# Prompt values of one attention pair: one full-array product per key block in place of two column-half products

## What is computed

```python
def sparse_attend(q, k_sel, v_sel, q_pos, k_pos, rel_bias):
    logits = jnp.einsum('bthd,btkhd->bhtk', q, k_sel).astype(jnp.float32) * ATTN_SCALE
    ...
    p = jax.nn.softmax(logits, axis=-1).astype(v_sel.dtype)
    out = jnp.einsum('bhtk,btkhd->bthd', p, v_sel)
    return out.reshape(q.shape[0], q.shape[1], D_ATTN)
```

## Time and profile before

| | |
|---|---|
| three executions | 1859.91, 1866.31, 1863.84 us; median 1863.84 |
| profiled execution | span 1871.8 us from the first to the last instruction; what lies around the span is not shown by its profile |
| TensorE busy | 1726.3 us (92%) |
| VectorE, ScalarE, GpSimd busy | 859.4, 653.4, 603.9 us |
| stage with the changed line | 539 to 966 us of the span |

### The profile page before, as it was taken

One profiled execution on the slowest core, in us unless ns is written; L12 is line 12 of the kernel. 1 busy time (PEld: TensorE's weight loads), 2 busy tenths in 40 slices (PEclk: granted clock), 3 DMA queues, 4 the chain that ended last, 5 costly groups with the idle time before them and its releaser, 6 DMA issues.

```text
span 1871.8 us, 28982 instructions
## 1 busy us (share of the span) xinstructions
PE 1726.3 (92%) x11176; PEld 1413.1 (75%) x11176; DVE 859.4 (46%) x1839; ACT 653.4 (35%) x1374; POOL 603.9 (32%) x715
## 2 busy tenths in 40 slices
PE   7888999989967778898789999999999999999998
PEld 6553464789944455565555689999999999999997
DVE  4571889757734444566531343323132323232324
ACT  4464786577232233343321121222222222222123
POOL 1100334266354665555513140404040404040400
PEclk9799999989987899998889999999999999999999
DMA  8301202111184655655571001111110101020202
GB/s 242 93 1 49 92 31 78 49 35 42 43 270 149 177 173 160 175 152 152 149 260 66 0 1 46 46 46 45 39 50 29 60 20 70 10 80 3 98 1 96
DMA packets 68965, 158.03 MB, mean 84 GB/s; under 512 B 9402, under 2 KB 25518, under 8 KB 68608
## 3 DMA queue, kind: packets, MB, share of 16 engines
q1 hardware_dynamic: 47488, 84.91, 13.7%
q0 software_dynamic: 21376, 71.75, 12.8%
HBM read 144.14 MB, written 12.49 MB: 84 GB/s over the span
## 4 chain that ended last, share of the span: by engine, by line
PE 82%; DVE 6%; issue 4%; another core or an unknown queue 3%; ACT 3%; POOL 2%; DMA 1%; SPq 0%; DVEq 0%; ACTq 0%; POOLq 0%
PE psum L1819 7%; PE psum L1817 7%; PE psum L1806 7%; PE psum L1807 7%; PE psum L1805 7%; PE psum L1818 7%; PE psum L1746 6%; PE psum L1360 5%; PE psum L1524 4%; PE psum L1373 3%; PE psum L1549 2%; PE psum L1663 2%; PE psum L1340 2%; PE psum L1641 2%
## 5 line engine op out<-in xcount | busy, mean ns | idle before, releaser
L1805 PE MATMUL psum<-n_hi,wup_hi 128*128 128x384 f32 (+1 forms) x768 | 251.3, 327 | 0.0
L1817 PE MATMUL psum<-h_hi,wdn_hi 128*128 128x384 f32 (+1 forms) x768 | 250.9, 327 | 0.0
L1807 PE MATMUL psum<-n_hi,wup_lo 128*128 128x384 f32 (+1 forms) x768 | 250.8, 327 | 0.0
L1806 PE MATMUL psum<-n_lo,wup_hi 128*128 128x384 f32 (+1 forms) x768 | 250.8, 327 | 0.0
L1819 PE MATMUL psum<-h_hi,wdn_lo 128*128 128x384 f32 (+1 forms) x768 | 250.2, 326 | 0.0
L1818 PE MATMUL psum<-h_lo,wdn_hi 128*128 128x384 f32 (+1 forms) x768 | 250.1, 326 | 0.0
L2441 DVE TENSOR_TENSOR h_lo<-h_full,h_hi 128x384 fp32r<-128x384 f32 (+1 forms) x96 | 112.5, 1184 | 261.5 <-ACT h_hi L1221 252.8
L1213 ACT ACTIVATE hrelu<-psum 128x384 f32<-128x384 f32 (+1 forms) x96 | 45.5, 474 | 502.0 <-PE psum L1807 502.0
L2446 DVE TENSOR_TENSOR x_region<-psum,x_region 128x384 f32<-128x384 f32 (+1 forms) x192 | 102.8, 536 | 252.9 <-PE psum L1819 251.8
L905 POOL TENSOR_TENSOR wup_lo<-wup_full,wup_hi 128x4096 fp32r<-128x4096 f32 x8 | 72.3, 9037 | 421.0 <-ACT wup_hi L1197 421.0
L1075 ACT ACTIVATE arena<-x_region,arena 128x384 bf16<-128x384 f32 (+2 forms) x192 | 166.5, 871 | 23.3 <-POOL arena L851 23.3
(11 more groups left out here) (329 smaller groups left out, 3155.1 us busy)
## 6 DMA issues: line engine op xcount, KB each, us to landing
wup_full<-in_w_up SPq DMA_DIRECT2D x8, 2048.0 KB, 8.0
wdn_full<-in_w_down SPq DMA_DIRECT2D x8, 2048.0 KB, 7.7
arena<-in_x_prompt SPq DMA_DIRECT2D x16, 512.0 KB, 8.8
arena<-in_w_in SPq DMA_DIRECT2D x3, 2048.0 KB, 8.4
arena<-in_w_in SPq DMA_DIRECT2D x12, 512.0 KB, 5.6
out<-arena SPq DMA_DIRECT2D x17, 256.0 KB, 4.5
arena<-in_w_out SPq DMA_DIRECT2D x8, 512.0 KB, 8.4
out<-arena SPq DMA_DIRECT2D x8, 512.0 KB, 2.7
```

Of the source, the lines that this page charges most:

```text
L1805: pe.matmul(b, wu_hi[:, k, col], n_hi[:, k, o:o + w], start=(k == 0), stop=False)
L1806: pe.matmul(b, wu_hi[:, k, col], n_lo[:, k, o:o + w], start=False, stop=False)
L1807: i = pe.matmul(b, wu_lo[:, k, col], n_hi[:, k, o:o + w], start=False, stop=(k == KT - 1))
L1817: pe.matmul(b, wd_hi[:, f, col], h_hi[:, hf, 0:w], start=(f == 0), stop=False)
```

## The change

For each key block of a pair there is one product: the 128 value columns of both heads as weights, and the 2 x 128 queries of both heads as moving columns, into all 128 partitions and 256 columns of bank 3. Of the four quarters of the result two are a head's own (partitions 0 to 63 with columns 0 to 127, partitions 64 to 127 with columns 128 to 255); the other two pair one head's values with the other head's probabilities and are not read. `take_values` copies the two own quarters, with one copy each. `pv_done` counts one a pair, and the waits on it are adapted.

```diff
@@ sync engine: loads of the output weights
-            sp.wait_ge(pv_done, 2 * NPR)
+            sp.wait_ge(pv_done, NPR)
@@ def even_turn(q, e), ScalarE
-                act.wait_ge(pv_done, 2 * q)
+                act.wait_ge(pv_done, q)
@@ def values(q), TensorE
                 for k in range(i_ + 1):
-                    for e in range(2):
-                        i = pe.matmul(bank(3)[64 * e:64 * e + 64, 0:P], V[:, k, (2 * hp + e) * HD:(2 * hp + e + 1) * HD],
-                                      probT[:, e, k, :], start=(k == 0), stop=(k == i_), skip_group_check=True)
-                        if k == i_:
-                            i.then_inc(pv_done, 1)
+                    i = pe.matmul(bank(3)[:, 0:2 * P], V[:, k, 2 * hp * HD:(2 * hp + 2) * HD], probT[:, :, k, :],
+                                  start=(k == 0), stop=(k == i_), skip_group_check=True)
+                i.then_inc(pv_done, 1)
@@ def odd_turn(q, e), VectorE
-                dve.wait_ge(pv_done, 2 * q)
+                dve.wait_ge(pv_done, q)
@@ def take_values(q), VectorE
-                dve.wait_ge(pv_done, 2 * q + 2)
-                dve.tensor_copy(mixT[:, hp, i_ * P:(i_ + 1) * P], bank(3)[:, 0:P]).then_inc(val_taken, 1)
+                dve.wait_ge(pv_done, q + 1)
+                for e in range(2):
+                    own = slice(64 * e, 64 * e + 64)
+                    i = dve.tensor_copy(mixT[own, hp, i_ * P:(i_ + 1) * P], bank(3)[own, e * P:(e + 1) * P])
+                i.then_inc(val_taken, 1)
```

## The result

Eight executions of each kernel were timed: 1865.8 us before, 1873.04 us after (medians), 7.2 us more; the ratio is 1.0041 with a 95% interval of 1.0022 to 1.0060, which is 7.6 us (4.1 to 11.2) of 1865.8. The forecast was +23.4, with 1871 to 1898 us for the median. The median lies inside that range, but the change is a third of what was forecast.

The account below looks back on a forecast made before the run. TensorE was taken to bound the kernel, with 87.5 us of holes in the stage from 539 to 966 us. Products +26.8, copies +1.6 and holes -5 gave +23.4 us: 1887 from 1863.8, range 1871 to 1898.

Parts of the forecast that it names:

- the price of the products: TensorE's value products at full clock: 38.7 us before, 62.8 after, so +24.1 us, bounds +19 to +31.
- the copies: VectorE's second value copy, exposed at eight waits before L1582: +1.6 us, between 0 and 9.
- Together -5: TensorE's stage: -4 us for fewer instructions plus -1 for longer bursts eating into holes behind them.
- What the holes give back: TensorE's idle time in the stage, 539 to 966 us, absorbs some added time: -5 us in sum.
- with the low stretches where they are: Value bursts partly at low clock: 24.1 us times 1.11 makes +26.8 us.
- half hidden: Rival: TensorE's holes swallow 10 to 20 of 28 us, leaving +8 to +18, say 1877 us; chance 0.17 for +6 to +16.
- not slower, by the clock: Rival: unbroken TensorE streaming keeps 2.4 GHz and ends the dips; all gone gives -14, 1850 us; chance of faster 0.05.
- the dips would stay because the holes stay: Stage's clock: dips follow holes of several us, which the change doesn't mend; about 100 us at 1.2 GHz.
- a clock of the stage that leaves 0.85 to 0.91: Sign of being wrong: the granted clock in the stage, 0.85 and 0.90 in its two parts before, leaves this range.
- 20 to 28 more: Profile after: distance from first value product to last, 539.2 to 964.1 us before, longer by 20 to 28 us.
- 1.1 to 1.6 us: Growth of each burst in the stage's second part; if all eaten from the holes behind, about 20 us.

Follow-up runs that it names:

- copies_only: Kernel of before, products unchanged, only the copy of the values split in two of 64x128: 1780.89 us against 1775.83, ratio 1.0023.
- one_copy: Changed kernel's full-array products, but one 128x128 copy as before (part of the output not computed): 1790.66 us against 1775.83 for the kernel of before, ratio 1.0085.
- before_again: Kernel of before, unaltered, profiled a second time; first value product to first product of the output projection: 430.8 us.
- after_again: Changed kernel, unaltered, profiled a second time in the same job as before_again; first value product to first product of the output projection: 438.1 us.
- before_few: Kernel of before with each gather from the ninth tile of each ring on replaced by a plain transfer of 16 rows: 1767.91 us against 1875.38.
- after_few: Changed kernel with the same plain transfers for gathers as before_few: 1791.71 us against 1875.38 for the kernel of before, ratio 0.9553.
- before_light: Kernel of before with gathers from the ninth tile of each ring on fetching 64 instead of 512 columns, as many rows: 1861.40 us against 1867.16.
- after_timed: Changed kernel, unaltered, timed again on another chip: 1872.39 us against 1875.38 for the kernel of before, ratio 0.9982.
- after_light: Changed kernel with the same light gathers as before_light: 1871.18 us against 1867.16 for the kernel of before, ratio 1.0026.

## Why the prediction was off

**Right: the price of the products.** 0.22 us a key block before, 0.216 us a record after (I took 0.218), which makes the 24.1 us at full clock. With the gathers away the whole change measured 23.8, on chips with short holes 18.3.

**Right in kind, too small: the copies.** I had 1.6 us and a bound of 9; copies_only measured 5.1. The place was the named one: the wait before L1582 is 10.6 us in copies_only and 7.0 in one_copy.

**Wrong: what is given back.** The step that failed is "Together -5" under *What the holes give back*, and with it "with the low stretches where they are", which multiplied the price by 1.11. On the chips with long holes a change that costs 23.8 us without gathers ended as +7.6, -3.0, +9.8 (with light gathers) and, by the second profiles, +7.3. So 14 to 27 us came back where I had 5.

The two pairs of profiles show where. Before to after, the stage grew by 7.3 us with gathers (before_again, after_again) and by 23.3 without (before_few, after_few, on another chip of the same kind). Each column stands on one profile of either kernel:

| | with gathers | without | given back |
|---|---|---|---|
| TensorE's holes | -5.4 | +2.6 | 8.0 |
| the products' line | +30.7 | +28.4 | -2.3 |
| TensorE's other lines | -18.0 | -7.7 | 10.3 |
| the stage | +7.3 | +23.3 | 16.0 |

So half of the 16.0 us lies in the holes and half in TensorE's busy time. The second half is the clock: the stage had 99.0 us at 1.2 GHz before and 78.5 after, 13.7 and 10.2 without gathers (clocks of 0.980 and 0.986), and half of the 17 us between the two savings is 8.5. The other profiles on such chips agree: 99 us in the first profile and in before_light, 75, 68 and 72 in the first profile after, after_timed and after_light. Most of the 7.7 us that the other lines lose even without gathers belongs to the ends of the bursts: before the change 0.20 us pass from the start of the last transpose to the burst, with it 0.11, and the longer last record of a burst covers 0.17 us of the next line's time instead of 0.07.

The first timing went the way I said; that of after_timed did not. The rival that came out was a mixture of *half hidden* and *not slower, by the clock*, to which I gave 0.17 and 0.05. I had argued that the dips would stay because the holes stay. My own sign of being wrong, a clock of the stage that leaves 0.85 to 0.91, was there: 0.94 in the second part of the first profile, 0.92 over the stage of after_timed. The first value product and the last lay 420.6 us apart in the first profile after for 424.9 before, where I had 20 to 28 more; the second pair has 423.7 for 415.1. One figure of the working is off without effect: by its own prices a burst of the last four query blocks grows by 0.9 to 1.5 us, not 1.1 to 1.6.

**Shown:** on a chip with long holes the holes belong to the gathers, not to their bytes or packets but to the gathers as such (before_light, before_few); without them the change costs nearly its full price; with them, on a chip with long holes, it came out 45.7 us ahead of column-half products that take 8 us more of TensorE. **Open:** by which property. Fewer instructions is one candidate, tried only where there are no long holes; the full array itself and the longer products are others. Open too is why the holes and the stretches at 1.2 GHz shrink together, and why chips differ.

The Trainium skill (Runtime: NRT & Kernel Launch, Instruction fetch mechanics) describes how engines stream their instructions in blocks by a DMA queue of their own and calls the cost mostly hidden. No run here shows that the holes are such fetches; if they were, that page's judgement would not hold beside these gathers. What the profiles show of such queues speaks against it: the larger one, `q8 instruction`, has 29 packets of about 1 us each in the stage of before_again and as many in that of before_few, and the 3 us behind each of them make up 20% of the stage of before_again and hold 16% of TensorE's holes. Only two such queues appear, so this doesn't settle it.

## What to carry to other kernels

A price per instruction read from start-to-start distances carried over well here; what a stage full of unexplained holes gives back did not. It deserves a range of its own, with the clock in it (here 14 to 27 us came back in a stage with some 80 us of holes and 99 us at 1.2 GHz), not a middle value. Two column-half fp32 products in alternation ran at the same time here, so one full-array product that computes both heads' cross terms doubled TensorE's time for a key block, 0.43 us for 0.22. Look for a second copy in front of the one place that waits at once, and put it where its engine is waiting anyway: that was worth 5.3 us to the kernel of before and 9.6 to the changed one.

## What was not expected of the hardware

The same program takes 1776 us on some chips and 1866 to 1875 on others, all of the difference in the stage with GpSimd's gathers; without these gathers a chip of the slower kind ran the kernel of before in 1768 us. Gathers of an eighth of the bytes changed 5.8 us, plain transfers of as few bytes in as many packets 107.5. Of the stage of before, 99 us ran at 1.2 GHz in each of three executions, while its holes went from 79 to 88 us. Wait instructions that are already fulfilled follow each other on TensorE by 0.106 us: 32 of them cost 2.4 us where the array has only a 1.9 us burst to run meanwhile, and some 0.3 us behind a burst of 3.5 us.
